# A decoder step on one core: cache keys of the decode part turned by VectorE in 32x32 blocks, scores in 32x32 tiles

## The chip, the core and the metric

The kernel runs on one of the eight cores of a Trainium2 chip. The metric is the time of one execution on the device in microseconds; before the change it is 4006.55 us, the median of three runs.

## What is computed

The reference is one inference step of a decoder layer for two inputs: a prompt of 2048 positions, and 8 sequences that decode 4 new positions each over a past of 8192. Both go through a projection, attention and an MLP; attention has two halves of four head pairs each. The decode part of attention, which the change touches, is cut here to its core:

```python
# dilated heads: keys at t, t-d, t-2d, ... of a window of the last 2048 positions
def dilated_branch_sample(q, k_all, v_all, window, dil):
    ...
    sc = jnp.einsum('nthe,ntjhe->nthj', q, kg).astype(jnp.float32) * (e ** -0.5)
    p, m, l = softmax_parts(sc, valid[None, :, None, :])
    o = jnp.einsum('nthj,ntjhe->nthe', p, vg.astype(jnp.float32)) / l
# differential heads: all keys of a paged cache, two maps per head
def diff_attention_core(q, k, v, valid, lam):
    sc = jnp.einsum('nqhce,nkhce->nhcqk', q, k).astype(jnp.float32) * (e ** -0.5)
    a = jax.nn.softmax(jnp.where(valid, sc, -jnp.inf), axis=-1)
    wts = a[:, :, 0] - lam * a[:, :, 1]
    return jnp.einsum('nhqk,nkhe->nqhe', wts, v.astype(jnp.float32))
```

A query row of decode is one of 4 positions, 4 head pairs and 2 heads or maps: 32 rows for each sequence and each half.

## The kernel before

The program has three stages one after the other: `project`, `attend` and `mlp`. All five engines are programmed by hand with semaphores; each carries out its own list in order.

`attend` does two things at once. The **prompt part** walks over units `u` (a tile of 128 queries; first 128 units of the dilated heads, then 64 of the differential heads) and their parts `j` of up to 512 keys. For each part TensorE makes scores (`scores`, L1000) for a unit that is two or three ahead, turns the probabilities of the present one (`turn_keys`, L1015) into one of the `turn` banks, and multiplies the copied ones with the values (`product`, L1050). VectorE adds the bias and takes the minimum (`biased`, L1394) and combines the two maps (`invert`, L1414), ScalarE does the exponentials (L1237) and copies turned tiles out of PSUM (`copies`, L1248; some of them fall to VectorE, `by_vector`).

The **decode part** walks over 8 sequences `n` and 9 chunks `c` of each: eight chunks of 8 pages of 128 cached positions for the differential heads, one chunk of eight 128-row groups of the window for the dilated ones; 72 chunks in all. For a chunk:
- SyncE loads the keys and GpSimd's queue the values in halves of 4 pages of 128 x 512 fp32 (rings `ck`, `cv` of three halves).
- TensorE turns the keys with 32 transposes of 128x128 (`turn_cache`, L1104), four to a bank; ScalarE (L1294) and VectorE (L1506) copy the banks in turn to `kT`.
- `cache_scores` (L1119) puts the scores into one bank: row 32 j + r is query row r against the keys of slot j (256 of the chunk's 1024 keys), summed over the four head pairs with queries that are zero outside their own head.
- VectorE takes the maximum of 256 columns (`maxima`, L1514, L1520, L1521), ScalarE the factor alpha for the old sum (L1303) and the exponentials (L1305).
- TensorE turns the 128x256 probabilities (`turn_prob`, L1130), ScalarE copies them (L1311), and `cache_values` (L1146) multiplies each slot with all 512 value columns; VectorE adds the result to `acc` (`add`, L1533).

Each query row so exists in four slots with its own maximum and sum. At the **edge** between two sequences (`edges`, seven steps) the four are brought to one maximum (L1156, L1160), their sums added (L1179), the finished sequence mixed (L1187), and the new positions' own keys scored (L1169) and their values taken (L1195, L1207).

The order between the two parts is fixed when the program is built. `pace` gives each prompt part a cost by its width and each decode step a cost from a table, and lays the decode steps between the parts so that both advance in proportion; every engine's list follows the same interleaving (`together`):

```python
turn, score, turn_p, value, edge = 0.46, 1.75, 0.3, 1.75, 1.0
chunk = [score, turn, turn, turn_p, turn, turn, value, turn, turn, turn, turn]
```

The turns of the next chunk's keys so stand between the steps of the present one.

Of the kernel before, what the change touches and what calls it, by code (L numbers as in the profile page):

```python
# [24 lines left out]
P = 128  # L25
# [404 lines left out]
SL = 4  # L430
# [4 lines left out]
def attend(nc, io, keep):  # L435
# [8 lines left out]
    TURNS, WB, OB, QB, KB, VB, CB = 3, 4, 2, 2, 6, 5, 5  # L444
    HK, HV = 3, 3
    H = CH // 2
    EV = NP * CH // 4
# [55 lines left out]
    def pace():  # L503
# [12 lines left out]
        turn, score, turn_p, value, edge = 0.46, 1.75, 0.3, 1.75, 1.0  # L516
        chunk = [score, turn, turn, turn_p, turn, turn, value, turn, turn, turn, turn]
        decode = [turn] * EV
        for n in range(ND + 1):
            decode += [edge] * 7 + (chunk * NC if n < ND else [])  # L520
# [21 lines left out]

    def chunk_after(n, c):
        return (n, c + 1) if c < NC - 1 else (n + 1, 0) if n < ND - 1 else None

    turn_keys_no, turn_inv_no, turn_coef_no, turn_cache_no, turn_prob_no, turn_new_no = {}, {}, {}, {}, {}, {}
# [9 lines left out]
    def by_vector(u, j, k):  # L556
        return not is_diff(u) and (k == 1 or (len(packs(u, j)) == 1 and u % 4 == 3))

    def count_prompt():
        for u in range(-AHEAD, NU):  # L560
            for j in steps(u):
# [3 lines left out]
                if u >= 0 and j < n_parts(u):  # L565
                    for k in range(len(packs(u, j))):
                        use(turn_keys_no, (u, j, k), 1 if by_vector(u, j, k) else 0)
                    if is_diff(u) and u % OT == OT - 1 and j == n_parts(u) - 1:
                        use(turn_inv_no, (u - DIFF0) // OT, 0)
                yield  # L570

    def count_decode():
        def turns(which, es):
            for e in es:
                if which is not None:
                    use(turn_cache_no, (*which, e), e % 2)
                yield
        yield from turns((0, 0), range(EV))
        for n in range(ND + 1):
            for edge in range(7):  # L580
                if edge == 4 and n < ND:
                    use(turn_new_no, n, 1)
                yield
            for c in range(NC if n < ND else 0):
                yield
                yield from turns(chunk_after(n, c), range(0, 2))
                use(turn_prob_no, (n, c), 0)
                yield
                yield from turns(chunk_after(n, c), range(2, 4))
                yield  # L590
                yield from turns(chunk_after(n, c), range(4, EV))
# [3 lines left out]
    with ExitStack() as ctx:  # L595
# [38 lines left out]
        kT = sb("c_kT", [P, NP, CH * P])  # L634
        q_rows = sb("c_q_rows", [P, 2, NP, SL * ROWS])
        v_new = sb("c_v_new", [TD, 2, GW])
        bias_new = sb("c_bias_new", [P, 2, TD])
        bias_win = sb("c_bias_win", [P, 2 * P])
        own_head = sb("c_own_head", [P, 2, GW])
        same_row = sb("c_same_row", [P, P])  # L640
        token = sb("c_token", [P, TD])
# [5 lines left out]
        s_win = sb("c_s_win", [P, 2 * P])  # L647
        m = sb("c_m", [P, 2, 2])
        chunk_max = sb("c_chunk_max", [P, 1])
        c_shift = sb("c_shift", [P, 2])  # L650
        shift_new = sb("c_shift_new", [P, 2])
        alpha = sb("c_alpha", [P, 2])
        l_new = sb("c_l_new", [P, 2])
        l_chunk = sb("c_l_chunk", [P, 2])
        l = sb("c_l", [P, 2])
        prob = [sb(f"c_prob{i}", [P, 2 * P]) for i in range(2)]
        pT = [sb(f"c_pT{i}", [P, 2 * P]) for i in range(2)]
        acc = sb("c_acc", [P, 2, GW])
        m_row = sb("c_m_row", [2, ROWS])
        m_rows = sb("c_m_rows", [2, SL, ROWS])  # L660
        below = sb("c_below", [P, 2])
        weight = sb("c_weight", [P, 2])
        lw = sb("c_lw", [P, 2])
        coef = sb("c_coef", [P, 2])
        comb = sb("c_comb", [P, 2, TD])
# [4 lines left out]
        cs_ps, co_ps = ps("c_s"), ps("c_o_ps")  # L670
        X_T = 2 * P
        X_M, X_L, X_O = X_T + P, X_T + P + 4, X_T + P + 8
# [29 lines left out]
        co_full, co_added, l_added = sem("c_o_full"), sem("c_o_added"), sem("c_l_added")  # L702
        new_scored, new_shifted, new_exped = sem("c_new_scored"), sem("c_new_shifted"), sem("c_new_exped")
# [1632 lines left out]
```

## Time and profile before

| | |
|---|---|
| three runs | 4004.82, 4006.55, 4008.26 us |
| profiled execution | 4008.4 us, span of its instructions 4006.8 us |
| TensorE (PE) busy | 3703.2 us, 92% |
| VectorE (DVE) busy | 2360.9 us, 59% |
| ScalarE (ACT) busy | 1570.7 us, 39% |
| mean granted TensorE clock | 0.957 |
| `attend` | about 741 to 2257 us |
| `mlp` | from 2257 us to the end |

PE's row counts matmuls, PEld the loading of their weights beside them. A group of instructions has a line, its tiles (written <- read), a count, its busy time and the idle time of the engine just ahead of it, with what ended that. The granted clock is a share of full speed.

### The profile page before, as it was taken

The page shows a single profiled execution, that of the slowest core. Times are in us where ns is not written, and L with a number is a line of the kernel's source. Part 1 is how long each engine was busy: PE and PEld are TensorE (multiplying, and loading weights), DVE is VectorE, ACT ScalarE, POOL GpSimd, SP SyncE. Part 2 cuts the span into 40 slices and gives each one's busy share as a digit, 9 for nine tenths or more (in the row PEclk, how much of TensorE's full clock was granted, in tenths as well). Part 3 has the DMA queues.
Part 4 walks back from the last instruction along what each step waited for, and adds up shares of the span by engine and source line. Part 5 has one row for each costly group of instructions (what it writes and reads, how often), then busy time and mean ns, then how long its engine had stood idle before and what let it go on. Part 6 is the DMA issues. An engine that isn't in the chain of part 4 may idle for free. (4 is left out here: it accounts for less than half of the span.)

```text
span 4006.8 us, 69226 instructions
## 1 busy us (share of the span) xinstructions
PE 3703.2 (92%) x24074; PEld 3143.2 (78%) x24074; DVE 2360.9 (59%) x5009; ACT 1570.7 (39%) x3039; POOL 356.3 (9%) x615
## 2 busy tenths in 40 slices
PE   7997799698989988989898699999999999999998
PEld 6885687466766666666666499999999999999998
DVE  4444343264555566666666566767767676676665
ACT  2222122253544443544444344444434434443433
POOL 0003000021212121222212000000000000000000
PEclk9998899698989998999989899999999999999999
DMA  5785763686868676867667344335434434433432
GB/s 176 250 280 176 262 220 109 189 277 205 281 199 285 210 267 205 277 198 281 213 224 240 112 150 134 115 114 155 119 93 150 136 104 139 146 114 110 140 113 70
DMA packets 529360, 725.20 MB, mean 181 GB/s; under 512 B 45688, under 2 KB 355192, under 8 KB 528025
## 3 DMA queue, kind: packets, MB, share of 16 engines
q1 hardware_dynamic: 480057, 502.32, 40.5%
q0 software_dynamic: 48128, 218.14, 15.9%
q8 instruction: 178, 2.92, 0.3%
q14 instruction: 133, 1.09, 0.1%
q10 hardware_dynamic: 864, 0.73, 0.1%
HBM read 653.30 MB, written 134.61 MB: 197 GB/s over the span
## 5 line engine op out<-in xcount | busy, mean ns | idle before, releaser
L2157 DVE TENSOR_TENSOR d_y<-d_y,d_dps 128x416 f32<-128x416 f32 x640 | 371.9, 586 | 246.5 <-PE d_dps L1822 246.5
L1820 PE MATMUL d_dps<-d_u_hi,d_down_hi 128*128 128x416 f32 x1280 | 459.1, 359 | 11.6 <-DVE d_y L2157 11.6
L1822 PE MATMUL d_dps<-d_u_hi,d_down_lo 128*128 128x416 f32 x1280 | 452.5, 353 | 0.0
L1822 PE MATMUL d_ups<-d_h_hi,d_up_lo 128*128 128x416 f32 x1280 | 451.0, 352 | 0.0
L1820 PE MATMUL d_ups<-d_h_hi,d_up_hi 128*128 128x416 f32 x1280 | 450.2, 352 | 0.0
L1821 PE MATMUL d_dps<-d_u_lo,d_down_hi 128*128 128x416 f32 x1280 | 448.8, 351 | 0.0
L1821 PE MATMUL d_ups<-d_h_lo,d_up_hi 128*128 128x416 f32 x1280 | 446.9, 349 | 0.0
L1104 PE MATMUL turn<-ident,c_k 128*128 128x128 f32 x2304 | 322.4, 281 | 42.5 <-DMA c_k<-in_k_cache 14.8
L761 POOL DMA_DIRECT2D c_v<-in_v_cache x512 | 276.8, 541 | 941.2 <-issue 941.2
L1104 PEld LDWEIGHTS turn<-ident,c_k 128*128 128x128 f32 x2304 | 256.4, 143 | 111.1 <-issue 51.4
L408 PE MATMUL a_zps<-a_w_hi,a_xT_hi 128*128 128x512 f32 (+1 forms) x816 | 330.3, 405 | 10.6 <-DVE a_w_lo L337 7.5
L410 PE MATMUL a_zps<-a_w_hi,a_xT_lo 128*128 128x512 f32 (+1 forms) x816 | 327.3, 401 | 0.0
L409 PE MATMUL a_zps<-a_w_lo,a_xT_hi 128*128 128x512 f32 (+1 forms) x816 | 324.9, 398 | 0.0
L1506 DVE COPY c_kT<-turn 128x512 f32<-128x512 f32 x288 | 197.7, 690 | 175.7 <-PE turn L1104 175.2
L2099 DVE TENSOR_TENSOR d_up_lo<-d_up_raw,d_up_hi 128x1024 fp32r<-128x1024 f32 x200 | 244.1, 1221 | 96.3 <-ACT d_up_hi L1943 96.1
L1248 ACT COPY b_wT<-turn 128x512 f32<-128x512 f32 (+2 forms) x264 | 138.7, 525 | 321.7 <-PE turn L1015 321.0
L1820 PEld LDWEIGHTS d_dps<-d_u_hi,d_down_hi 128*128 128x128 f32 x1280 | 241.6, 189 | 17.5 <-DVE d_y L2157 13.3
L1949 ACT CAST d_down_hi<-d_down_raw 128x2048 fp32r<-128x2048 f32 x80 | 152.7, 1908 | 253.9 <-PE d_dps L1822 253.6
L1943 ACT CAST d_up_hi<-d_up_raw 128x1024 fp32r<-128x1024 f32 x200 | 208.1, 1041 | 98.3 <-PE d_ups L1822 95.7
L1821 PEld LDWEIGHTS d_dps<-d_u_lo,d_down_hi 128*128 128x128 f32 x1280 | 241.8, 189 | 6.0 <-issue 2.6
L1821 PEld LDWEIGHTS d_ups<-d_h_lo,d_up_hi 128*128 128x128 f32 x1280 | 240.4, 188 | 4.4 <-issue 0.8
L1822 PEld LDWEIGHTS d_dps<-d_u_hi,d_down_lo 128*128 128x128 f32 x1280 | 241.3, 189 | 1.9
(215 smaller groups left out, 6759.2 us busy)
## 6 DMA issues: line engine op xcount, KB each, us to landing
c_v<-in_v_cache POOLq DMA_DIRECT2D x512, 256.0 KB, 5.2
c_k<-in_k_cache SPq DMA_DIRECT2D x512, 256.0 KB, 4.5
d_up_raw<-in_w_up SPq DMA_DIRECT2D x160, 512.0 KB, 4.3
d_down_raw<-in_w_down SPq DMA_DIRECT2D x80, 1024.0 KB, 5.5
out_ka_win<-in_ka_state POOLq DMA_DIRECT2D x8, 4064.0 KB, 15.5
out_va_win<-in_va_state POOLq DMA_DIRECT2D x8, 4064.0 KB, 27.1
d_up_raw<-in_w_out SPq DMA_DIRECT2D x40, 512.0 KB, 3.9
a_x<-in_x_prompt SPq DMA_DIRECT2D x32, 512.0 KB, 4.8
```

The lines of the kernel that those rows point to most:

```text
L408: nc.tensor.matmul(dst, x_hi, w_hi[i][:, c, :], start=(c == 0), stop=False)
L409: nc.tensor.matmul(dst, x_hi, w_lo[i][:, c, :], start=False, stop=False)
L410: m = nc.tensor.matmul(dst, x_lo, w_hi[i][:, c, :], start=False, stop=(c == KC - 1))
L761: eng.dma_start(dst[:, g, :], io[src[0]][bass.ds(page, 1)].rearrange("o p d -> (o p) d")).then_inc(landed, 16)
L1104: ins = nc.tensor.transpose(turn[n % TURNS][:, g * P:(g + 1) * P], ck[h % HK][:, g, p * P:(p + 1) * P], keep["ident"][:])
L1506: nc.vector.tensor_copy(kT[:, e % 4, e // 4 * 512:(e // 4 + 1) * 512], turn[n % TURNS][:]).then_inc(copied[1], 1)
L1820: nc.tensor.matmul(dst, w_hi, x_hi, start=first, stop=False)
L1821: nc.tensor.matmul(dst, w_hi, x_lo, start=False, stop=False)
L1822: return nc.tensor.matmul(dst, w_lo, x_hi, start=False, stop=last)
L1943: nc.scalar.copy(up_hi[n % UB][:], up_raw[n % 2][:]).then_inc(up_hi_ready, 1)
L2099: nc.vector.tensor_tensor(up_lo[n % UB][:], up_raw[n % 2][:], up_hi[n % UB][:].bitcast(F32), ALU.subtract).then_inc(up_lo_ready, 1)
L2157: nc.vector.tensor_tensor(part, part, d_ps[k % DB][:, 0:W], ALU.add).then_inc(d_used, 1)
```

## The change

Only the decode part of `attend` and its constants change.

- **Keys.** The 32 transposes and the 8 copies of a chunk go. VectorE turns the keys itself, from SBUF to SBUF, with four instructions of 128x1024 (`turn_cache`), each of which transposes all 32x32 blocks in place. Head dimension block x of a pair then lies on 32 partitions for each block k of 32 keys in a page.
- **Scores.** `cs_ps` has two banks. Each head pair has 32 rows of its own, of which 8 are used; each block k of 32 partitions holds a quarter of the keys. A score is summed over four 32x32 tiles x: 64 matmuls of 32 x 32 x 256 in place of 16 of 128 x 32 x 256. Blocks 0 and 2 come first, then, behind a wait of TensorE for its own half (`cs_half`), blocks 1 and 3.
- **Softmax.** A query row is one row, so slots have no longer to be joined. Maximum and exponentials run over 1024 columns instead of 256.
- **Values.** Eight transposes turn the 128x1024 probabilities; 32 matmuls of 128 x 32 x 128 take only the pair's own value columns; `acc` is 128x128 for each kind.
- **Edges** have four steps instead of seven; mixing takes two matmuls instead of eight.
- **Banks and order.** `TURNS` goes from 3 to 2, `by_vector` goes (ScalarE makes all copies of the prompt's turned tiles), and `pace` has a new table.

```diff
-    TURNS, WB, OB, QB, KB, VB, CB = 3, 4, 2, 2, 6, 5, 5
+    TURNS, WB, OB, QB, KB, VB, CB = 2, 4, 2, 2, 6, 5, 5
...
-        turn, score, turn_p, value, edge = 0.46, 1.75, 0.3, 1.75, 1.0
-        chunk = [score, turn, turn, turn_p, turn, turn, value, turn, turn, turn, turn]
+        edge = 1.5
+        chunk = [3.0, 1.5, 1.3, 1.0, 1.9, 0.5]
...
+    KEY_STEPS = (1, 2, 3, 5)
...
                 def cache_scores(n, c):
+                    i, kd = n * NC + c, kind(c)
+                    pe.wait_ge(keys_turned, EV * (i + 1))
+                    wait(pe, c_exped, i)
+                    for pair_of_blocks in ((0, 2), (1, 3)):
+                        for x in range(4):
+                            for k in pair_of_blocks:
+                                rows = slice(k * BLK, (k + 1) * BLK)
+                                for p in range(NP):
+                                    at = (p * 4 + x) * BLK
+                                    ins = nc.tensor.matmul(
+                                        cs_ps[ROWS * p:ROWS * (p + 1), k * 2 * P:(k + 1) * 2 * P],
+                                        q_rows[rows, kd, p, x, :], kT[rows, :, at:at + BLK],
+                                        start=(x == 0), stop=(x == 3))
+                        if pair_of_blocks == (0, 2):
+                            ins.then_inc(cs_half, 1)
+                            pe.wait_ge(cs_half, i + 1)
+                    ins.then_inc(cs_full, 1)
...
-                    for p in range(NP):
-                        for j in range(SL):
-                            ins = nc.tensor.matmul(
-                                cs_ps[ROWS * j:ROWS * (j + 1), 0:2 * P],
-                                q_rows[:, kind(c), p, ROWS * j:ROWS * (j + 1)],
-                                kT[:, p, j * 2 * P:(j + 1) * 2 * P], start=(p == 0), stop=(p == NP - 1))
...
-                    for a in range(2):
-                        for j in range(SL):
-                            g = 2 * j + a
+                    for g in range(CH):
+                        for p in range(NP):
                             ins = nc.tensor.matmul(
-                                co_ps[ROWS * j:ROWS * (j + 1), :], pT[i % 2][:, a * P + ROWS * j:a * P + ROWS * (j + 1)],
-                                cv[(2 * i + g // H) % HV][:, g % H, :], start=(a == 0), stop=(a == 1))
+                                co_ps[ROWS * p:ROWS * (p + 1), 0:P], pT[:, g * P + ROWS * p:g * P + ROWS * (p + 1)],
+                                cv[(2 * i + g // H) % HV][:, g % H, p * P:(p + 1) * P], start=(g == 0), stop=(g == CH - 1))
...
+                def turn_cache(which, e):
...
+                    i = which[0] * NC + which[1]
+                    h = i * 2 + e // 2
+                    if e % 2 == 0:
+                        dve.wait_ge(ck_in[h % HK], half_landed(h, HK))
+                    wait(dve, cs_full, i)
+                    pages = slice(e % 2 * 2, e % 2 * 2 + 2)
+                    nc.vector.transpose(kT[:, e * 2:e * 2 + 2, :].rearrange("p g d -> p (g d)"),
+                                        ck[h % HK][:, pages, :].rearrange("p g d -> p (g d)")).then_inc(keys_turned, 1)
...
                     if kd:
-                        link(nc.vector.tensor_reduce(chunk_max[:], cs_ps[:, 0:2 * P], AX.X, ALU.max))
+                        link(nc.vector.tensor_reduce(chunk_max[:], cs_ps[:], AX.X, ALU.max))
```

How this moves TensorE's list shows chunk 60, in the differential half: from its scores (`c_s`) to its turned probabilities. `b_` names are the prompt part. Before:

```order
L1119 MATMUL c_s<-c_kT,c_q_rows 32x256 x16
L1000 MATMUL b_s<-b_k_hi,b_q_hi 128x384 x2
L1000 MATMUL b_s<-b_k_lo,b_q_hi 128x384 x2
L1000 MATMUL b_s<-b_k_hi,b_q_lo 128x384 x2
L1015 MATMUL turn<-ident,b_w 128x128
L1050 MATMUL b_ops<-b_wT,b_v 128x128 x4
L1104 MATMUL turn<-ident,c_k 128x128 x8
L1000 MATMUL b_s<-b_k_hi,b_q_hi 128x512 x2
...
L1015 MATMUL turn<-ident,b_w 128x128 x4
L1050 MATMUL b_ops<-b_wT,b_v 128x128
L1130 MATMUL turn<-ident,c_prob 128x128 x2
```

and after:

```order
L1089 MATMUL c_s<-c_kT,c_q_rows 32x256 x64
L984 MATMUL b_s<-b_k_hi,b_q_hi 128x512 x2
L984 MATMUL b_s<-b_k_lo,b_q_hi 128x512 x2
L984 MATMUL b_s<-b_k_hi,b_q_lo 128x512 x2
L999 MATMUL turn<-ident,b_w 128x128 x4
L1034 MATMUL b_ops<-b_wT,b_v 128x128
L1106 MATMUL turn<-ident,c_prob 128x128 x8
```

Eight key transposes and one of the two prompt parts no longer stand between the two. The second place is VectorE's list at the end of the same chunk, up to the maximum of the next one. Before:

```order
L1533 SCALAR_TENSOR_TENSOR c_acc<-c_acc,c_alpha,c_o_ps 128x512 [waits c_o_full]
L1394 ISA b_w,b_part<-b_s,b_bias_causal 128x512 [waits b_s_full]
L1394 ISA b_part 128x1
...
L1506 COPY c_kT<-turn 128x512 [waits c_s_full,turned] x2
L1394 ISA b_w,b_part<-b_s,b_bias_causal 128x512 [waits b_s_full]
...
L1514 TENSOR_REDUCE c_chunk_max<-c_s 128x1 [waits c_s_full]
```

and after:

```order
L1489 SCALAR_TENSOR_TENSOR c_acc<-c_acc,c_alpha,c_o_ps 128x128 [waits c_o_full]
L1350 ISA b_w,b_part<-b_s,b_bias_causal 128x512 [waits b_s_full]
L1350 ISA b_part 128x1
...
L1454 STREAM_TRANSPOSE c_kT<-c_k 128x1024 [waits c_s_full]
L1462 TENSOR_REDUCE c_chunk_max<-c_s 128x1 [waits c_s_full]
```

The last key transpose now stands directly ahead of the maximum, behind the prompt part's tiles; TensorE's scores of the next chunk wait for it.

## Rows read from the trace of the kernel before

**Rows 1.** Busy time by stretch: us, each engine busy (x instructions), granted clock, DMA share, GB/s.
```profile
741.00:1395.00 654.00, 597.92 (x5563) 422.01 (x5563) 354.04 (x1115) 297.78 (x900) 124.32 (x229) 0.91 0.74 236
1395.00:2257.00 862.00, 766.67 (x6503) 547.19 (x6503) 535.36 (x1548) 386.55 (x796) 181.26 (x333) 0.94 0.69 231
741.00:2257.00 1516.00, 1364.59 (x12066) 969.20 (x12066) 889.40 (x2662) 684.33 (x1696) 305.58 (x562) 0.93 0.71 233
2257.00:4007.00 1750.00, 1694.67 (x9010) 1660.80 (x9010) 1171.24 (x1569) 726.38 (x1061) 0.00 (x0) 0.98 0.41 124
```

**Rows 2.** Groups by line, PE, 741 to 2257 us: busy us, mean ns, idle before, releasers.
```profile
L1104 PE MATMUL turn<-ident,c_k 128*128 128x128 f32 x2304 | 322.4, 281 | 42.5 <-DMA c_k<-in_k_cache 14.8 <-DVE c_kT L1506 8.4 <-ACT c_kT L1294 8.3
...
L1119 PE MATMUL c_s<-c_kT,c_q_rows 128*32 128x256 f32 x2304 | 144.7, 393 | 37.7 <-issue 29.4 <-ACT c_kT L1294 8.3
L1146 PE MATMUL c_o_ps<-c_v,c_pT 128*32 128x512 f32 x1152 | 138.5, 598 | 0.4 <-ACT c_pT L1311 0.4
...
L1130 PE MATMUL turn<-ident,c_prob 128*128 128x128 f32 x144 | 29.2, 284 | 16.6 <-ACT c_prob L1305 9.1 <-ACT b_wT L1248 6.2 <-ACT c_kT L1294 0.9
L1207 PE MATMUL c_o_ps<-c_v_new,c_pT_new 4*128 4x512 f32 x32 | 28.8, 994 | 14.9 <-DVE c_acc L1623 12.1 <-DVE c_pT_new L1617 2.8
L1187 PE MATMUL c_s<-c_comb,c_acc 128*128 128x4 f32 x128 | 23.2, 313 | 2.1 <-DVE c_comb L1602 2.1
...
L1169 PE MATMUL c_s<-ksT,c_q_rows 128*128 128x4 f32 x128 | 21.8, 302 | 6.0 <-DVE c_below L1576 6.0
```

**Rows 3.** Timeline of PE from 2230 us: start us, us, engine, line, tiles, xcount.
```profile
2230.46 1.93 PE L1119 MATMUL c_s<-c_kT,c_q_rows 128*32 128x256 f32 x32 [0.83 <-ACT c_kT L1294]
2232.32 0.50 PE L1000 MATMUL b_s<-b_k_hi,b_q_hi 64*128 64x512 f32 x2
...
2233.22 0.44 PE L1015 MATMUL turn<-ident,b_w 128*128 128x128 f32 x2
2233.49 1.06 PE L1050 MATMUL b_ops<-b_wT,b_v 128*128 128x128 f32 x8
...
2238.64 1.92 PE L1146 MATMUL c_o_ps<-c_v,c_pT 128*32 128x512 f32 x16
```

**Rows 4.** Timeline of PE from 747 us, eight transposes of keys at full clock.
```profile
747.61 1.04 PE L1104 MATMUL turn<-ident,c_k 128*128 128x128 f32 x8
```

**Rows 5.** Groups by line, DVE, 741 to 2257 us.
```profile
L1506 DVE COPY c_kT<-turn 128x512 f32<-128x512 f32 x288 | 197.7, 690 | 175.7 <-PE turn L1104 175.2
L1394 DVE CUSTOM_DVE_ANT_0 b_w<-b_s,b_bias_causal 128x512 f32<-128x512 f32 x224 | 145.7, 688 | 37.1 <-PE b_s L1000 33.0 <-issue 0.5
...
L1533 DVE SCALAR_TENSOR_TENSOR c_acc<-c_acc,c_alpha,c_o_ps 128x512 f32<-128x512 f32 x72 | 53.7, 746 | 77.7 <-PE c_o_ps L1146 77.5
...
L1514 DVE TENSOR_REDUCE c_chunk_max<-c_s 128x1 f32<-128x256 f32 x64 | 27.2, 424 | 108.1 <-PE c_s L1119 108.1
...
L1520 DVE TENSOR_TENSOR c_m<-c_m,c_chunk_max 128x1 f32<-128x1 f32 x72 | 11.5, 160 | 2.5
...
L1581 DVE TENSOR_TENSOR c_acc<-c_acc,c_own_head 128x1024 f32<-128x1024 f32 x8 | 9.7, 1218 | 0.0
```

**Rows 6.** Groups by line, ACT, 741 to 2257 us.
```profile
L1294 ACT COPY c_kT<-turn 128x512 f32<-128x512 f32 x288 | 167.5, 584 | 163.5 <-PE turn L1104 161.3
L1248 ACT COPY b_wT<-turn 128x512 f32<-128x512 f32 x184 | 107.4, 583 | 230.9 <-PE turn L1015 230.4
...
L1305 ACT ACTIVATE c_prob<-c_s,c_shift 128x256 f32<-128x256 f32 x64 | 29.2, 456 | 0.0
...
L1303 ACT ACTIVATE c_alpha<-c_m,c_shift 128x1 f32<-128x1 f32 x72 | 21.2, 295 | 241.3 <-DVE c_shift L1521 241.3
...
L1237 ACT ACTIVATE b_w<-b_w,b_shift 128x1024 f32<-128x1024 f32 x8 | 9.2, 1153 | 0.0
```

**Rows 7.** Timeline of 0.12 us at the start of the same score group.
```profile
2230.43 0.19 PEld L1119 LDWEIGHTS c_s<-c_kT,c_q_rows 128*32 128x32 f32 x8 [1.04 <-ACT c_kT L1294]
2230.46 0.42 PE L1119 MATMUL c_s<-c_kT,c_q_rows 128*32 128x256 f32 x4 [0.83 <-ACT c_kT L1294]
```

More of the change, by code:

```diff
@@ L429 @@
 CH = 8
-SL = 4
 ROWS = 32
@@ L572, in count_decode @@
     def count_decode():
[L573 to L578, printed above, removed]
+        for e in range(EV):
+            yield
         for n in range(ND + 1):
-            for edge in range(7):
-                if edge == 4 and n < ND:
+            for edge in range(EDGES):
+                if edge == 2 and n < ND:
                     use(turn_new_no, n, 1)
@@ L584, in count_decode @@
             for c in range(NC if n < ND else 0):
[L585 to L591, printed above, removed]
+                for step in range(6):
+                    if step == 2:
+                        for a in range(2):
+                            use(turn_prob_no, (n, c, a), 0)
+                    yield
     together(count_prompt(), count_decode())
@@ L652, in attend @@
         alpha = sb("c_alpha", [P, 2])
-        l_new = sb("c_l_new", [P, 2])
         l_chunk = sb("c_l_chunk", [P, 2])
         l = sb("c_l", [P, 2])
[L656 to L663, printed above, removed]
+        prob = sb("c_prob", [P, CH * P])
+        pT = sb("c_pT", [P, CH * P])
+        acc = sb("c_acc", [P, 2, P])
         coef = sb("c_coef", [P, 2])
-        comb = sb("c_comb", [P, 2, TD])
+        comb = sb("c_comb", [P, 2, NP * TD])
         s_ps = [ps(f"b_s{i}") for i in range(2)]
@@ L1132, in turn_prob @@
-                    ins.then_inc(turned, 1)
+                        t = turn_prob_no[n, c, a]
+                        after_copy(pe, t - TURNS)
+                        for g in range(H):
+                            at = (a * H + g) * P
+                            ins = nc.tensor.transpose(turn[t % TURNS][:, g * P:(g + 1) * P], prob[:, at:at + P],
+                                                      keep["ident"][:])
+                        ins.then_inc(turned, 1)
                 def cache_values(n, c):
@@ L1286, in prompt @@
                             yield
-                def copy_keys(which, es):
-                    for e in es:
-                        if which is not None and e % 2 == 0:
-                            i, n = which[0] * NC + which[1], turn_cache_no[(*which, e)]
-                            act.wait_ge(turned, n + 1)
-                            wait(act, cs_full, i)
-                            nc.scalar.copy(kT[:, e % 4, e // 4 * 512:(e // 4 + 1) * 512], turn[n % TURNS][:]).then_inc(copied[0], 1)
-                        yield
                 def cache_exps(n, c):
```

370 lines of the change are left out of this document (155 added, 215 removed).

## Prediction

> **What bounds the kernel now.** I read the stretches first [rows 1]. The attention stage, from 741 to 2257 us, is the only one that the change touches: 1516 us, TensorE (PE) busy for 1365 of them, VectorE (DVE) 889, ScalarE (ACT) 684, DMA at 0.71. In its first 654 us the dilated heads of the prompt run beside 30 of the 72 chunks of cache, in the other 862 us the differential heads beside 42 chunks. The stage after it, 1750 us, stays as it is. So PE's time in the stage is what has to be summed, with a check whether DVE, which takes work over, becomes the one waited for. The groups of PE's lines say what the decode part costs there [rows 2]; the timeline says how long one such piece lasts at full clock [rows 3, 4]; DVE's and ACT's groups price their pieces [rows 5, 6].
>
> **PE, what goes.** Busy time and the idle time ahead of it count together [rows 2]. The 2304 transposes of cache keys (L1104): 322.4 + 42.5 = 365 us. The scores (L1119): 144.7 + 37.7 = 182. The values (L1146): 139. The transposes of probabilities (L1130): 29.2 + 16.6 = 46. The edges between sequences, their three large groups (L1207, L1187, L1169): 43.7 + 25.3 + 27.8 = 97; the small ones are left out on both sides. Together 829 us.
>
> **PE, what comes.** An fp32 matmul is two passes in the trace (1152 score matmuls in the program, 2304 records). Today 32 passes of 256 columns, on four column groups at a time, take 1.93 us [rows 3], and one pass takes 393 ns [rows 2]: eight waves, so a wave costs (1.93 - 0.39) / 7 = 0.22 us. The changed scores are 64 matmuls of 32x32, 128 passes. They are written so that row groups 0 and 2, then 1 and 3, work beside each other on four column groups: eight tiles at a time, 16 waves. The wait on c_s_half in the middle cuts them into two blocks of eight waves, each as long as today's block: 3.86 us. With the entry of 37.7 / 72 = 0.52 us that is 4.38 us a chunk, 315 us. If the row groups don't overlap it is 32 waves (a rival below). The values stay four tiles wide, 64 passes of 128 columns instead of 16 of 512; the columns streamed are the same, so I take the same 139 us. Probabilities: eight transposes instead of two, 1.04 us [rows 4], 75 us. Edges: two mixing matmuls for eight (a quarter of 25.3 us), half of the 28 us of the new scores, and about half of the 44 us of the new values, since two round trips to DVE become one: 6 + 14 + 24 = 44 us. Together 573 us. Without new waits PE gains 829 - 573 = **256 us**.
>
> **What the waits take back.** The cache transposes were also filler: PE did them while DVE and ACT worked on the scores. The order of chunk 60 shows it: between its scores and its turned probabilities stand now two prompt parts and eight key transposes, afterwards one part with a single product. Take T as the end of the scores.
> - DVE's maximum over 1024 columns instead of 256: copies and products of 512 and 1024 columns differ by (1218 - 690) / 512 = 1.03 ns a column [rows 5], so 424 + 768 x 1.03 = 1.22 us, then two small operations of 0.16 us (L1520 and one like it). ACT then needs 0.30 us for alpha and about 1.15 us for 1024 exponentials, as its 1024-column row [rows 6]. The probabilities are there at T + 3.1 us, against 0.42 + 0.32 + 0.30 + 0.46 = T + 1.5 now.
> - PE's one part is 0.90 us of scores, four transposes of 0.11 (eight take 1.04) and two passes of 0.11 of product [rows 3, 4]: T + 1.6. It waits 1.5 us.
> - DVE goes on: two biased tiles of 0.69 us with their read-outs (1.5), two key transposes, one more part, a third transpose, the sum. The 128x1024 transpose of 32x32 blocks is in no row. The nearest is L1581, a 128x1024 operation from SBUF to SBUF at 1218 ns; the bounds are 0.69 us (the 512-column copy) and 2.44 us (two passes over the data). I take 1.22. That brings DVE to T + 9, the next part's tiles to T + 10.7, the fourth transpose to T + 11.9. PE, which has done turned probabilities, part, values and part, stands at T + 10.4 and waits 1.5 us for c_keys_turned. What is queued behind that wait on PE is the whole prompt.
>
> So a tight chunk of three parts pays 3.0 us. A chunk has 4.4 parts on average (315 parts, 72 chunks), and where a second part stands in the gap the wait goes. I take 2.0 us a chunk, 144 us; bounds 0.5 (36 us, hardly more than the 16.6 us that L1130 waits now) and 3.5 us (252 us).
>
> **DVE and the rest.** DVE loses the key copies (288 x 0.69 = 198 us) and gains 288 x 1.22 = 351, loses 0.4 and gains 1.22 us a chunk on the maximum, and its sum shrinks from 0.75 to about 0.3 us a chunk. With some of the prompt's copies going to ACT (each 0.58 us there, [rows 6]) it ends near 1000 of some 1400 us. It also idles while PE does scores, today 108 us [rows 5], then some 3.7 us a chunk, 270 us: nearly full in the second half, which is why I don't take the low bound of the waits. ACT loses 168 us of key copies [rows 6] and gains less than that: no cost; it only adds to waits where a long prompt exponential stands ahead. Two transpose buffers instead of three cost nothing, because the third held key tiles; were that cover missing, a part would pay a copy of 0.58 us. The key loads (SP) now wait for DVE's transposes, the value loads (POOL) for the same values as before; nothing else stands behind them, and DMA goes from 0.71 to 0.76 of its time.
>
> **Sum.** The profiled execution took 4008.4 us for a span of 4006.8, 1.9 us above the median of the three runs. 4008.4 - 256 + 144 = **3896 us**. Its own range, from the bounds of the waits: 3788 to 4004.
>
> **Rivals.**
> - **Row groups don't overlap.** Each half of the scores then has 16 waves: 2 x (15 x 0.22 + 0.39) = 7.4 us, 3.5 more a chunk, +253: **4149 us**, slower. For it: no row shows two 32-row tiles at work. Against it: today's prompt scores use two 64-row groups, and two matmuls of 512 columns are done within 0.50 us there [rows 3], where a single wave of 512 columns in fp32 takes 0.44. It decides as soon as a block of 32 matmuls lasts over 2.9 us. The Trainium skill (TensorEngine Tiling (Array Packing), Gotcha 1: PSUM Pressure) says that different row tiles cannot use one PSUM bank at once. By it nothing is lost here, since blocks 0 and 2 write to different halves of a two-bank tile; no run so far shows it. Chance 0.10.
> - **PE's issue binds.** If 1.93 / 32 = 60 ns a pass is the rate at which instructions come, and not that of the array, the scores take 128 x 0.06 = 7.7 us and the values 3.8: +276 and +138 us, **4310 us**. Against it: eight weight loads and four matmuls start within 0.12 us [rows 7]. The Trainium skill (TensorE: Matmul & The Clock Gate, Part 2) gives about 62 ns of sequencer time per matmul with hardware decode off; by that rule the scores would need 7.9 us. Row and rule differ, and I follow the row. Chance 0.03.
> - **The DVE transpose costs two passes, 2.44 us.** In the tight chunk the fourth transpose ends 4.6 us later and PE waits for it; over a mean chunk I take 3 us, +216: **4112 us**, slower. It decides from about 1.9 us for one transpose. The Trainium skill (Vector Engine (DVE) Microarchitecture Reference, 3.8) says that the transpose sustains one element per cycle and lane, which is on the side of my 1.22 us; no row shows it. Chance 0.12.
> - **Every chunk is tight**, with an exponential of the prompt in front as well: 3.5 us a chunk, **4004 us**, no change. Chance 0.06.
>
> **How the numbers follow.** The forecast has 0.69. A measurement of this kernel can tell about 0.2% (8 us) from no change. Faster: 0.69. Within 0.2%: 0.05 of the last rival. Slower: 0.10 + 0.03 + 0.12 + 0.01 = 0.26. The range runs from the forecast's low end, 3785, to just over the third rival, 4120; it leaves out the first two rivals and a little below, under 0.2.
>
> **What would show it.** Right: the 128-pass score group at some 3.9 us, blocks of eight matmul starts together; the DVE transpose near 1.2 us; PE idle ahead of c_prob and of c_s, waiting for c_prob (ACT) and c_kT (DVE), 2 us a chunk together; a stage of about 1404 us. Wrong: a score group over 6 us, a transpose over 1.9 us, waits beyond 3.5 us a chunk, or a granted clock below the present 0.93 in the stage. The stage of 1750 us should not move.

## The result and the profile after

| | before | changed |
|---|---|---|
| median | 4005.7 us (4 runs) | 4098.7 us (4 runs) |
| span of the profiled execution | 4006.8 us | 4101.7 us |
| attention stage | 1516 us | 1613 us |
| TensorE busy, idle in it | 1365, 151 us | 1353, 260 us |
| granted clock in it | 0.93 | 0.84 |

The changed kernel is slower: ratio 1.0235, interval 1.0214 to 1.0257. Here and below a ratio is that of medians, against the kernel before as measured beside the run, with its 95% interval; those medians of the kernel before lie between 4005.2 and 4007.9 us. The forecast was 3896 us. The profiled execution took 4103.3 us; 207 us are missing.

The stretches after, with the columns of [rows 1]:

```profile
741.00:1395.00 654.00, 566.62 (x8566) 401.49 (x8566) 367.36 (x1037) 275.01 (x816) 117.90 (x218) 0.82 0.71 227
1395.00:2354.00 959.00, 786.53 (x11950) 581.09 (x11946) 640.63 (x1598) 367.49 (x706) 186.38 (x344) 0.86 0.64 215
741.00:2354.00 1613.00, 1353.15 (x20510) 982.59 (x20510) 1007.99 (x2635) 642.51 (x1520) 304.29 (x562) 0.84 0.67 220
2354.00:4102.00 1748.00, 1694.71 (x9010) 1660.80 (x9010) 1170.85 (x1566) 726.03 (x1061) 0.00 (x0) 0.98 0.41 123
```

The last stage did not move. In the attention stage TensorE is busy for 12 us less, where the sum had 173 less, and the granted clock is 0.84 instead of 0.93. PE's groups after, 741 to 2354 us (to compare with [rows 2]):

```profile
L1089 PE MATMUL c_s<-c_kT,c_q_rows 32*32 32x256 f32 x9216 | 348.0, 441 | 55.3 <-DVE c_kT L1454 41.5 <-issue 4.8 <-PE c_s L1089 0.3
L999 PE MATMUL turn<-ident,b_w 128*128 128x128 f32 x1112 | 214.7, 322 | 29.7 <-DVE b_w L1370 16.0 <-DVE b_o_near L1401 8.6 <-ACT c_pT L1268 2.8
L1034 PE MATMUL b_ops<-b_wT,b_v 128*128 128x128 f32 x1088 | 174.4, 308 | 7.4 <-ACT b_wT L1208 7.2
L1122 PE MATMUL c_o_ps<-c_v,c_pT 128*32 128x128 f32 x4608 | 145.6, 280 | 10.0 <-ACT c_pT L1268 8.7 <-issue 1.3
L1106 PE MATMUL turn<-ident,c_prob 128*128 128x128 f32 x576 | 95.3, 313 | 25.6 <-ACT c_prob L1260 14.0 <-ACT b_wT L1208 11.4
L984 PE MATMUL b_s<-b_k_hi,b_q_hi 64*128 64x512 f32 x248 | 72.2, 574 | 51.1 <-DVE b_part L1350 42.4 <-DVE b_shift L1350 7.7 <-DVE b_both L1350 0.9
...
L1166 PE MATMUL c_o_ps<-c_v_new,c_pT_new 4*32 4x128 f32 x128 | 7.1, 352 | 4.3 <-DVE c_pT_new L1555 4.3
L1146 PE MATMUL c_o_ps<-c_comb,c_acc 128*128 128x16 f32 x32 | 6.9, 334 | 12.8 <-DVE c_comb L1543 12.8
...
L1135 PE MATMUL c_o_ps<-ksT,c_q_new 128*32 128x4 f32 x128 | 3.0, 194 | 39.1 <-DVE c_q_rows L1514 39.1
```

The reader is to see three things. The prompt's own groups, which the change did not touch, take longer: turning the prompt's probabilities (L999, before L1015) 214.7 us for 195.9, the products 174.4 for 155.3. TensorE now waits for DVE in many places: for keys (41.5), for bias tiles (b_part, 42.4 for 11.3 before), and for c_q_rows, the copies of the queries at the edges (39.1). The kernel before makes such copies too, 16 a sequence, but there they keep DVE busy for half as long, and TensorE never waits for them:

```profile
L1558 DVE COPY c_q_rows<-qsT 64x16 f32<-64x16 f32 x128 | 11.5, 174 | 0.3
```

And the scores are 348 us where the sum had 278 without their entry.

The timeline of PE after, two chunks:

```profile
2220.07 6.57 PE L1089 MATMUL c_s<-c_kT,c_q_rows 32*32 32x256 f32 x128 [2.00 <-DVE c_kT L1454]
2241.92 4.04 PE L1089 MATMUL c_s<-c_kT,c_q_rows 32*32 32x256 f32 x128
```

and the first 0.13 us of the second group:

```profile
2241.92 0.44 PE L1089 MATMUL c_s<-c_kT,c_q_rows 32*32 32x256 f32 x8
```

Eight tiles start together, so row groups do overlap. At full clock a group takes 4.04 us, near the 3.86 of the sum; the other one took 6.57 us, because the clock fell while it ran: TensorE is busy from 2220.07 us on, with a granted clock of 0.66 up to 2223.00 and of 0.50, the low level (1.2 GHz), from there to 2226.60. DVE's groups after, 741 to 2354 us, the counterparts of [rows 5], and ACT's exponential of [rows 6]:

```profile
L1454 DVE STREAM_TRANSPOSE c_kT<-c_k 128x1024 f32<-128x1024 f32 x286 | 346.6, 1231 | 7.8 <-DMA c_k<-in_k_cache 7.5 <-issue 0.3
...
L1462 DVE TENSOR_REDUCE c_chunk_max<-c_s 128x1 f32<-128x1024 f32 x64 | 78.4, 1225 | 288.8 <-PE c_s L1089 288.8
L1489 DVE SCALAR_TENSOR_TENSOR c_acc<-c_acc,c_alpha,c_o_ps 128x128 f32<-128x128 f32 x72 | 25.0, 347 | 81.4 <-PE c_o_ps L1122 81.3
...
L1514 DVE COPY c_q_rows<-qsT 32x32 f32<-32x32 f32 x128 | 22.6, 177 | 1.6
```

```profile
L1260 ACT ACTIVATE c_prob<-c_s,c_shift 128x1024 f32<-128x1024 f32 x64 | 70.1, 1095 | 0.0
```

The block transpose takes 1.23 us and the maximum 1.23 us, as priced; DVE idles 289 us in front of the maximum, as priced (270).

**Where the 207 us are**, by groups (busy; idle ahead), the profile after against the sum. In the rows on waits c_s and c_prob stand for the groups of the scores and of the turned probabilities:

| term | sum | measured | difference |
|---|---|---|---|
| scores, busy | 278 | 348 | +70 |
| prompt's 18 groups, busy | 875, as before | 943 | +68 |
| turned probabilities and values | 75 + 139 | 95 + 156 | +37 |
| edges | 44 | 73 | +29 |
| waits: c_s, c_prob, and what the prompt's groups wait more than their 28 us before | 38 + 144 | 55 + 26 + 78 | -23 |
| overlap: the groups' busy times add up to more than PE's | 0 | 232 before, 200 after | +32 |
| small groups of the edges, left out on both sides | 0 | 26 before, 5 after | -21 |
| a wait for the first keys, ahead of 741 us | -13 | 0 | +13 |

The overlap is an error of method. Each matmul group starts before the one ahead has drained, so the groups of before sum to 1597 us where PE was busy for 1365; a part of what I took away group by group was never there to gain. The last row is a misreading: of the 42.5 us of idle time taken away with L1104, 12.9 lie before the stage begins, and the changed kernel waits there for something else.

```profile
740.92 1.11 PE L1104 MATMUL turn<-ident,c_k 128*128 128x128 f32 x4 [12.93 <-DMA c_k<-in_k_cache]
```

The eight rows make 205 us; the rest is rounding and some 1 us of the last stage.

### The profile page after: what moved, and what is told of

Read it like the earlier page. It is cut to its first block and busy times, and to the rows that moved or that the text cites. A ratio compares the mean times of both kernels' runs of the same rounds, so it can differ in the third digit from the quotient of the medians.

```text
span 4101.7 us, 85450 instructions
## 1 busy us (share of the span) xinstructions
PE 3694.1 (90%) x32530; PEld 3158.1 (77%) x32530; DVE 2482.6 (61%) x4986; ACT 1530.5 (37%) x2871; POOL 354.9 (9%) x615
## 5 line engine op out<-in xcount | busy, mean ns | idle before, releaser
L1759 PE MATMUL d_dps<-d_u_hi,d_down_hi 128*128 128x416 f32 x1280 | 458.8, 358 | 11.3 <-DVE d_y L2096 11.3
L1089 PE MATMUL c_s<-c_kT,c_q_rows 32*32 32x256 f32 x9216 | 348.0, 441 | 55.3 <-DVE c_kT L1454 41.5
L1454 DVE STREAM_TRANSPOSE c_kT<-c_k 128x1024 f32<-128x1024 f32 x288 | 349.1, 1231 | 15.6 <-DMA c_k<-in_k_cache 15.3
L1089 PEld LDWEIGHTS c_s<-c_kT,c_q_rows 32*32 32x32 f32 x9216 | 181.9, 118 | 190.5 <-issue 53.0
L1208 ACT COPY b_wT<-turn 128x512 f32<-128x512 f32 (+3 forms) x320 | 164.8, 526 | 320.7 <-PE turn L999 320.1
L1462 DVE TENSOR_REDUCE c_chunk_max<-c_s 128x1 f32<-128x1024 f32 x64 | 78.4, 1225 | 288.8 <-PE c_s L1089 288.8
```

Of the source, the lines that this page charges most:

```text
L1089: ins = nc.tensor.matmul(cs_ps[ROWS * p:ROWS * (p + 1), k * 2 * P:(k + 1) * 2 * P], q_rows[rows, kd, p, x, :], kT[rows, :, at:at + BLK], s ...
L1454: nc.vector.transpose(kT[:, e * 2:e * 2 + 2, :].rearrange("p g d -> p (g d)"), ck[h % HK][:, pages, :].rearrange("p g d -> p (g d)")).then ...
L1759: nc.tensor.matmul(dst, w_hi, x_hi, start=first, stop=False)
```

## The experiments

Theories first. **A**: the granted clock fell because the 32-row score tiles hold half of the array while they run. **B**: it fell because TensorE now stands in waits that the key transposes used to fill. What TensorE waits for is a question apart.

**pad64.** 64-row tiles; the half of the weights that belongs to the other block is zero.

```diff
-rows = slice(k * BLK, (k + 1) * BLK)
+rows = slice(k // 2 * HD, (k // 2 + 1) * HD)
-q_rows[rows, kd, p, x, :], kT[rows, :, at:at + BLK]
+q_rows[rows, k % 2, kd, p, x, :], kT[rows, :, at:at + BLK]
```

> The changed kernel with its scores in tiles of 64 rows instead of 32: the weights of the other block's 32 rows are zero, the same 64 matmuls, the same eight tiles at a time, the same waits, the same scores; only the rows of the array that a tile takes are doubled (all 16 of its 32x32 parts instead of 8). Theory A (the granted clock of the attention stage fell from 0.93 to 0.84 because the score tiles hold only half of the array for 3.9 us a chunk): clock of the stage back to 0.91 to 0.94, TensorE's busy time in it down by 90 to 130 us, time about 3990 (3970 to 4010). Theory B (it fell because TensorE now stands in waits of 110 us more, which the key transposes used to fill): clock stays at 0.84, time 4090 to 4105. Score group 3.9 us in both.

Measured: 4055.6 us, ratio 1.0115 (1.0098 to 1.0132). Its stage, and the groups of PE in it, 741 to 2306 us:

```profile
741.00:2306.00 1565.00, 1262.71 (x20510) 939.24 (x20510) 1007.54 (x2635) 641.03 (x1520) 304.29 (x562) 0.91 0.69 227
```

```profile
L1089 PE MATMUL c_s<-c_kT,c_q_rows 64*32 64x256 f32 x9216 | 305.3, 400 | 55.2 <-DVE c_kT L1454 41.5 <-issue 4.6 <-PE c_s L1089 0.5
L999 PE MATMUL turn<-ident,b_w 128*128 128x128 f32 x1112 | 199.9, 305 | 37.0 <-DVE b_w L1370 19.8 <-DVE b_o_near L1401 9.2 <-ACT c_pT L1268 4.8
...
L1106 PE MATMUL turn<-ident,c_prob 128*128 128x128 f32 x576 | 92.4, 305 | 41.2 <-ACT c_prob L1260 23.4 <-ACT b_wT L1208 17.6
```

The clock went from 0.84 to 0.91 and busy time fell by 90 us, as theory A had it, with the very same waits in the program. The first score group of the stage shows it by itself. In the changed kernel TensorE is busy in it from 766.2 to 773.7 us, and the granted clock is 0.50 throughout; in pad64 it is 0.53 for the group's first 3.55 us and 1.00 for its last 1.96. B is out as the cause of this fall: TensorE is idle for 302 us here, more than the 260 of the changed kernel, and has the higher clock. But the time fell by 43 us only, outside A's range: 42 of the 90 us came back as idle time, because a faster TensorE reaches DVE's and ACT's results sooner (c_prob 14.0 to 23.4 us). The Trainium skill (TensorE: Matmul & The Clock Gate, What's actually happening) says that the gate follows how busy the engine has recently been. In the trace's sense of busy this pair goes the other way: 0.84 of the stage busy at clock 0.84, 0.81 busy at 0.91.

**full_rows.** The scores as 32 matmuls of 128 rows, four at a time.

```diff
-for k in pair_of_blocks:
+k = pair_of_blocks[x // 2]
...
-q_rows[rows, kd, p, x, :], kT[rows, :, at:at + BLK],
-start=(x == 0), stop=(x == 3))
+q_rows[:, kd, p, x, :], kT[:, :, at:at + BLK],
+start=(x % 2 == 0), stop=(x % 2 == 1))
```

> The changed kernel with its scores as 32 matmuls of all 128 rows and 32 columns, four at a time, two blocks of eight waves as now. What they compute is not the scores of the kernel; probabilities and values go on from them. Theory A: as pad64, clock 0.91 to 0.94 and time 3970 to 4010. Theory B: 4090 to 4105. If pad64 does not raise the clock and this does, it is rows with data that count, not rows that a tile takes (theory C).

Measured: 4045.3 us (1.0094, 1.0077 to 1.0111), clock 0.91 in the stage. The time is above A's range again. Rows filled with data do no more for the clock than pad64's rows of zeros, so theory C is out.

**before_32_rows.** The reverse, on the kernel before.

```diff
-q_rows[:, kind(c), p, ROWS * j:ROWS * (j + 1)],
-kT[:, p, j * 2 * P:(j + 1) * 2 * P], start=(p == 0), stop=(p == NP - 1))
+q_rows[0:ROWS, kind(c), p, ROWS * j:ROWS * (j + 1)],
+kT[0:ROWS, p, j * 2 * P:(j + 1) * 2 * P], start=(p == 0), stop=(p == NP - 1))
```

> The kernel before with its 16 score matmuls a chunk over the first 32 rows of queries and keys instead of all 128: the same number of matmuls, columns, waits and key transposes, so the same 1.93 us a chunk, with a quarter of the array. The scores lack three quarters of their sum. Theory A: the clock of the stage falls, from 0.93 to 0.89 to 0.91 (half as long as the change's scores, a quarter of the array), time 4030 to 4075. Theory B: nothing moves, clock 0.93, 3995 to 4012.

Measured: 4035.9 us (1.0077, 1.0058 to 1.0096). Its stage:

```profile
741.00:2281.00 1540.00, 1404.09 (x12062) 998.35 (x12060) 889.79 (x2665) 687.32 (x1696) 304.52 (x562) 0.90 0.71 230
```

With all key transposes and waits of the kernel before in place, 32-row tiles alone lower the clock from 0.93 to 0.90 and cost 29 us. That is A's direction and size.

**prob_turned_twice.**

```diff
-for g in range(H):
+for g in (*range(H), *range(H)):
```

> The changed kernel with its eight transposes of probabilities done twice, 1.04 us of full-array work more on TensorE in each of 72 chunks, 75 us in all (the same outputs). Theory A: the clock rises a little, to 0.85 to 0.87, which gives back 20 to 40 us; time 4110 to 4160. Theory B (filler is what is missing): the clock rises to 0.88 or more, and the time stays at 4080 to 4110 in spite of 75 us more work.

Measured: 4123.1 us (1.0290, 1.0273 to 1.0307), clock 0.87. 75 us of full-array work cost 24 us: busy time rose by 24 only, since the rest ran faster. A's numbers; the filler as such is not what is missing.

**pad64_no_wait.**

```diff
-if pair_of_blocks == (0, 2):
-    ins.then_inc(cs_half, 1)
-    pe.wait_ge(cs_half, i + 1)
```

> pad64 without the wait on c_s_half between the two blocks of scores, which 64-row tiles do not need (blocks 0 and 1 lie on the same rows). Theory D (each of the two blocks pays its pipeline once, 0.39 us a chunk): scores 3.5 to 3.6 us instead of 3.9 to 4.2, time 20 to 30 us under pad64, 4025 to 4035. Rival: DVE is as late as before, so what the scores save comes back as a longer wait for keys or for bias tiles: within 8 us of pad64, 4048 to 4064.

Measured: 4033.4 us (1.0069, 1.0053 to 1.0084), 22 us under pad64. Its timeline has the group at full clock as

```profile
2219.03 3.69 PE L1089 MATMUL c_s<-c_kT,c_q_rows 64*32 64x256 f32 x128
```

against 4.05 in pad64: 0.36 us x 72 = 26 us. Theory D holds in the time and at full clock, though 3.69 is a little more than the 3.5 to 3.6 expected; over all 72 groups the scores' busy time fell by 13 us only, from 305.3 to 292.4.

**pad64_queries_early.**

```diff
+if c == NC - 1 and n < ND - 1 and 1 <= step <= 4:
+    queries(n + 1, (step - 1,))
```

> pad64 with the 20 copies of a sequence's queries taken out of the edge, five in each of steps 1 to 4 of the last chunk of the sequence before it. Theory E (the prediction priced the edges' round trip but not these copies: 40 us of TensorE's idle time stand ahead of the new scores): that wait falls from 40 to under 15 us, time 25 to 35 us under pad64, 4020 to 4031. Rival: the copies now delay DVE's key transposes and the wait shows up at c_kT instead: within 8 us of pad64.

Measured: 4045.9 us (1.0103, 1.0088 to 1.0119), 10 us under pad64. The wait itself went as expected, from 40.3 to 11.7 us, but most of it was paid elsewhere (c_comb 12.8 to 21.7 us, and bias tiles). That lies between the two forecasts. Half right: the copies were an uncosted wait, but worth 10 us by the medians, not 30 (the profiled execution alone, with a span of 4029.6 us, was 24 under pad64's).

**pad64_keys_ahead** and **split_only.** The first splits the scores by pages and puts a key transpose between; the second splits the matmuls only.

```diff
+for half in range(2):
...
+at, to = (p * 4 + x) * BLK, k * 2 * P + half * P
-cs_ps[ROWS * p:ROWS * (p + 1), k * 2 * P:(k + 1) * 2 * P],
+cs_ps[ROWS * p:ROWS * (p + 1), to:to + P],
-q_rows[rows, k % 2, kd, p, x, :], kT[rows, :, at:at + BLK],
+q_rows[rows, k % 2, kd, p, x, :], kT[rows, half * H:(half + 1) * H, at:at + BLK],
```

In pad64_keys_ahead alone, TensorE waits for each half of the keys by itself, and of DVE's steps (the one of step 0 stands ahead of the maximum):

```diff
-wait(dve, cs_full, i)
+wait(dve, cs_full if e // 2 else cs_half, i)
-KEY_STEPS = (1, 2, 3, 5)
+KEY_STEPS = (0, 1, 2, 3)
```

> pad64 with the scores split by pages: first the 128 columns of the first four pages for all four blocks, then the other four, no wait between; DVE turns the first two pages of the next chunk's keys in between, ahead of the maximum instead of behind it, and the others one step earlier. Theory F (what costs the waits is the lock step: DVE stands idle for 3.9 us of scores in every chunk, 250 us, and its 349 us of key transposes are packed into the rest): DVE's idle time ahead of the maximum falls by 80 us or more, TensorE's idle time in the stage from 298 to 220 or less, time 3965 to 4005. Rival G (DVE is in time, and the waits are the chain scores, maximum, exponential, turned probabilities alone): only the saved c_s_half wait counts, 4025 to 4050.

> pad64_no_wait with each score matmul of 256 columns as two of 128 (128 matmuls a chunk instead of 64), all keys waited for ahead of them, DVE's order untouched. Theory I (the hole in pad64_keys_ahead is TensorE's instructions not arriving fast enough, since a group now has 512 of them; the idle time is put down to issue and to no wait): the same hole of 2.9 us, idle time ahead of the scores 180 to 200 us, time 4200 to 4250. Theory J (it came from the key transposes being ahead, by a wait on them): no hole, 4030 to 4060.

Measured: pad64_keys_ahead 4238.4 us (1.0579, 1.0563 to 1.0595), far on the wrong side of both theories. split_only 4324.6 us in a single run, so with no interval. PE's timeline in split_only:

```profile
2006.99 2.82 PE L1090 MATMUL c_s<-c_kT,c_q_rows 64*32 64x128 f32 x183 [0.23 <-DVE c_kT L1452]
...
2014.30 2.36 PE L1090 MATMUL c_s<-c_kT,c_q_rows 64*32 64x128 f32 x73 [4.49 <-issue]
...
2029.66 2.64 PE L1090 MATMUL c_s<-c_kT,c_q_rows 64*32 64x128 f32 x172 [1.70 <-DVE c_kT L1452]
2037.36 2.77 PE L1090 MATMUL c_s<-c_kT,c_q_rows 64*32 64x128 f32 x84 [5.06 <-issue]
```

Here are the same columns as in pad64, in twice the instructions, and a hole of 4 to 5 us after some 160 to 220 of 256 matmul records, in which no wait ends. Such holes are in most groups of both kernels: 79 in split_only, of 0.3 to 5.5 us and 227 us together, and 86 with 220 us in pad64_keys_ahead. So they are there with the key transposes ahead or not: J is out, and of I stands that the number of matmuls brings them, at a larger price than I gave it (4200 to 4250). The queues of DMA in the hole, 2009.8 to 2014.3 us, show one packet of instructions (the queue's 236 packets in this stage move 3.87 MB, 16 KB each):

```profile
q8 instruction: 1, 0.02, 1.3%
```

That instructions arrive too late is the reading that fits; it was not shown by itself, and the packet is weak evidence, as one comes every 8 us on average. The Trainium skill (Runtime: NRT & Kernel Launch, Instruction fetch mechanics) says that an engine fetches its program in blocks of 16 KiB and that this is mostly hidden; here, if the reading is right, it is not. The lock-step theory F could not be judged by the pair alone. Its sign did not come: DVE's idle time ahead of the maximum fell from 250.9 us in pad64 to 230.9 in pad64_keys_ahead, not by 80, and 161 us of new idle time stand ahead of the key transposes; but the holes lengthen both. Still, with the same matmuls, the kernel with the earlier key transposes was 86 us faster, by the one run of split_only.

**all_three.** pad64_keys_ahead with early queries.

> The three together: 64-row tiles, pages in halves with a key transpose ahead of the maximum, queries early. If theories A, D, E and F hold and add up: 3930 to 3975, faster than the kernel before. If F is wrong: 4000 to 4020.

Measured: 4222.2 us (1.0540, 1.0514 to 1.0567), 16 us under pad64_keys_ahead. It holds the same hole and settles nothing more.

**short_key_turns.**

```diff
-pages = slice(e % 2 * 2, e % 2 * 2 + 2)
+pages = slice(e % 2 * 2, e % 2 * 2 + (1 if i else 2))
```

> pad64_no_wait with each of DVE's key transposes over one page of two from the second chunk on: 284 operations of 512 columns instead of 1024, some 0.62 us less each, 175 us less DVE work; half of kT keeps the first chunk's keys, so scores, probabilities and values are not the kernel's. Theory F' (most of TensorE's 288 us of idle time in the stage is DVE being late, because its key transposes stand ahead of bias tiles and of the next scores): idle time falls by 90 us or more, time 3930 to 3960. Rival G (the idle time is the latency of the chain scores, maximum, exponential, turned probabilities): it falls by under 40 us, time 3995 to 4025.

Measured: 3987.7 us (0.9955, 0.9939 to 0.9971), 46 us under pad64_no_wait. Between the profiled executions, 51 us apart, TensorE's idle time falls by 30 us and its busy time by 19. Half-wide transposes took 697 ns, so DVE lost some 150 us of work. Idle time in G's range, time between the two: taking half of the transposes' work from DVE removes 30 of TensorE's 288 us of idle time. F' is out as the main cause; latency and order are left.

**no_wait_and_queries, more_in_the_gap, fourth_turn_sooner.** The first has the edits of pad64_no_wait and pad64_queries_early together; more_in_the_gap adds the first of these lines to it, fourth_turn_sooner the second.

```diff
-chunk = [3.0, 1.5, 1.3, 1.0, 1.9, 0.5]
+chunk = [3.0, 3.0, 1.3, 1.0, 1.9, 0.5]
...
-KEY_STEPS = (1, 2, 3, 5)
+KEY_STEPS = (1, 2, 3, 4)
```

> The two parts that helped, together: 64-row tiles without the wait between the blocks of scores, and queries copied early. If they add up: 4033 less 10 to 25, so 4008 to 4023, no faster than the kernel before.

> no_wait_and_queries with step 1 of a chunk (between scores and turned probabilities) counted as 3.0 instead of 1.5 in the table that lays prompt parts among the steps: more prompt work between scores and turned probabilities, less elsewhere. If the chain scores, maximum, exponential is what TensorE waits for, the wait at c_prob falls from 23 to under 10 us and the time by 10 to 30 us. If DVE is late for everything (F'), the wait only changes its place: within 8 us of no_wait_and_queries.

> no_wait_and_queries with the fourth key transpose in step 4 instead of step 5, before the last parts of the chunk and with the sum. If the fourth transpose is what the scores wait for (my tight chunk in the prediction): the wait at c_kT falls from 39 to under 20 us and the time by 10 to 20 us. If it is then paid at bias tiles (F'): within 8 us.

Measured: 4022.6 us (1.0043, 1.0031 to 1.0055); 4009.9 us (1.0011, 1.0002 to 1.0020); 4002.8 us (0.9995, 0.9984 to 1.0005). PE's groups of scores and turned probabilities, 741 to 2275 us, first in no_wait_and_queries:

```profile
L1089 PE MATMUL c_s<-c_kT,c_q_rows 64*32 64x256 f32 x9216 | 287.0, 397 | 47.9 <-DVE c_kT L1451 41.5 <-issue 5.9
...
L1103 PE MATMUL turn<-ident,c_prob 128*128 128x128 f32 x576 | 92.9, 306 | 40.8 <-ACT c_prob L1257 22.0 <-ACT b_wT L1205 18.2
```

in more_in_the_gap:

```profile
L1103 PE MATMUL turn<-ident,c_prob 128*128 128x128 f32 x576 | 91.7, 303 | 22.0 <-ACT c_prob L1257 12.4 <-ACT b_wT L1205 9.1
```

and in fourth_turn_sooner:

```profile
L1089 PE MATMUL c_s<-c_kT,c_q_rows 64*32 64x256 f32 x9216 | 278.9, 388 | 15.9 <-DVE c_kT L1451 11.1 <-issue 4.4
```

Both waits shrink where their cause was taken away (22.0 to 12.4, which is short of the "under 10" expected, and 41.5 to 11.1), and the time falls by 13 and 20 us. With the fourth transpose sooner this is idle time: TensorE's falls by 18 us in the stage, its busy time by 2. So that one is a wait of order, a key transpose that starts too late, which the prediction named. The other gain has a second source. In more_in_the_gap the wait for keys grows,

```profile
L1089 PE MATMUL c_s<-c_kT,c_q_rows 64*32 64x256 f32 x9216 | 282.6, 392 | 51.0 <-DVE c_kT L1451 47.0 <-issue 3.7
```

and idle time in all falls by 5 us only; busy time falls by 15, as the stage's granted clock goes from 0.91 to 0.93. The profiled execution was the fastest of its ten, so a part of this may be that execution's own. Why the clock moves with the order wasn't tested.

**both_orders, both_orders_wider, order_with_32_rows.** Both lines at once; the same with a wider table; and both lines with early queries on the changed kernel's 32-row tiles. The table of the second:

```diff
-chunk = [3.0, 3.0, 1.3, 1.0, 1.9, 0.5]
+chunk = [3.0, 3.0, 1.3, 1.0, 2.5, 1.5]
```

> no_wait_and_queries with both changes of order: more prompt work in the gap, and the fourth key transpose in step 4. If their gains (13 and 20 us) add: 3985 to 3995, faster than the kernel before by some 0.4%. If the wait only moves on once one of them is in: 4000 to 4006.

> both_orders with steps 4 and 5 counted as 2.5 and 1.5 instead of 1.9 and 0.5, so that more prompt work stands between the values and the next scores as well, and less beside the scores and the middle steps. If it is room before the next scores that DVE lacks: 5 to 15 us under both_orders. If the table is near its best: within 8 us, or slower.

> The changed kernel (32-row tiles, the wait between the blocks of scores) with queries early and both changes of order. If order and clock are separate costs: the order gives about as much as with 64-row tiles (10 + 33 us), 4050 to 4070, and the clock of the stage stays at 0.84 to 0.86. If at the low clock DVE has time enough and order matters less: 4070 to 4090.

Measured: 3992.9 us (0.9967, 0.9954 to 0.9980); 3991.0 us (0.9959, 0.9944 to 0.9975); 4051.1 us (1.0111, 1.0093 to 1.0129). The stages of both_orders and of order_with_32_rows:

```profile
741.00:2239.00 1498.00, 1230.83 (x20516) 944.81 (x20514) 1006.91 (x2636) 640.56 (x1524) 304.30 (x562) 0.93 0.72 237
```

```profile
741.00:2298.00 1557.00, 1309.88 (x20513) 966.17 (x20510) 1007.14 (x2636) 642.42 (x1522) 304.66 (x562) 0.88 0.69 228
```

The gains of the two orders add up (30 us of 33), about half of it in idle time and half in busy time (18 and 16 us of the stage against no_wait_and_queries), and the table is near its best. With 32-row tiles the order gives about as much (48 us with the queries), while clock and busy time stay behind: 58 us lie between the two, 22 of them the wait between the blocks. The clock did rise there, to 0.88, above the 0.86 that I allowed: order and clock are not separate costs. both_orders computes what the changed kernel computes and is 0.3% faster than the kernel before.

## Why the prediction was wrong

- **The step that failed: the granted clock, taken as it was.** The sum priced every group by durations at today's clock and had no term for the clock itself; it stood only among what would prove it wrong. pad64 puts its price at 90 us of busy time, 43 us of time with the waits as they were. It is the largest single cause found. It isn't the whole: pad64 still is 1.15% slower than the kernel before, and its stage is some 158 us over the sum's. By the rows of the table these are 38 of overlap, 34 of probabilities and values, 30 of edges, 27 of scores, 20 of waits, 17 of the prompt's groups and 13 of the first keys' wait, less the 21 of small groups. So the sum would have missed the sign with the clock in it. Scores in tiles of a quarter of the rows were costed by their length alone, 3.86 us; at full clock they took 4.04, and 4.83 on average (348 / 72).
- **Edges.** Priced by TensorE's groups [rows 2], 44 us; 73 measured, 39 of them behind the 20 small copies of queries a sequence on DVE (16 x 8 = 128 of them c_q_rows, 177 ns each), which the sum did not list. Such copies were there before, with no wait of TensorE behind them; what is new is their price, 28 us of DVE with the copies to c_q_new for 11.5, and that TensorE's next step waits for them. Worth 10 us when taken away.
- **Taking away by groups.** Group times overlap: 32 us of the difference could not be gained, nor could the 13 us of the wait ahead of the stage; the small groups of the edges, left out, give 21 back. One must take the difference of PE's busy time, not add groups.
- **Values and probabilities.** 37 us over: 10 are a new wait for the copy of c_pT. Low clock is little of the rest, since pad64, at 0.91, still has 92.4 us of turned probabilities and 146.8 of values. The sum took the full-clock 1.04 us for every group of eight transposes, where the mean of before was 1.12 (322.4 / 288). What remains isn't explained.
- **Waits.** 144 us were taken; with the scores' entry that makes 182 against 159 measured in the changed kernel and 202 in pad64. Right in size, and the two named waits are there: 41.5 us for c_kT, 25.6 ahead of the turned probabilities, each under the 1.5 us a chunk of the tight case. Half of the measured sum lies elsewhere, most of it ahead of the prompt's own scores, which wait for DVE's bias tiles. More of it was a matter of order than I saw: two numbers in the program give back 30 us, a part of them by the clock.
- **DVE.** Transpose 1.23 us for 1.22, maximum 1.23 for 1.22, busy 1008 for about 1000, idle ahead of the maximum 289 for 270. All right.
- **Rivals.** Row groups overlap; the issue of instructions does not bind at 64 matmuls a group. The DVE transpose is not two passes. "Every chunk is tight" is out too: with the scores' entry it needs 252 + 38 us of waits, and 159 were measured. None of the four contained the clock, so the range held the result, 4099, by the luck of another rival's 4112.

Still open: why the stage's clock also rises with the order of the work, from 0.84 to 0.88 with 32-row tiles. And what share of the 86 us between split_only and pad64_keys_ahead is the lock step of DVE and TensorE. A second buffer for the turned keys would tell; it wasn't tried. That the hole in split_only is a late block of instructions is argued, not shown.

## What to carry to other kernels

Before a full-array matmul is replaced by small tiles, put a term for the granted clock into the sum, over all that runs in that stage; if the tiles leave rows unused, zero-padded weights on taller tiles cost no time of their own and got 43 us back here. Work that is taken off the engine that bounds was also cover for the chains beside it: move the parts that lie in the gaps along with it, and take differences of the engine's busy time, not of its groups. And cost the small copies of a moved step on the engine that issues them.

## What the runs showed of the hardware

- Eight 32x32 or 64x32 tiles work at once into two PSUM banks: at full clock 16 waves of 256 columns take 4.04 us with a wait in the middle, and in 64x32 tiles 3.69 without it.
- The granted clock of the stage went with the rows that the score tiles take: 0.84 with 32 rows, 0.91 with 64 and with 128; on the kernel before 0.93 with 128 and 0.90 with 32. Rows with zero weights count like others. The order of the work moved it too, less: 0.84 to 0.88 with 32 rows, with early queries and both changes of order, and 0.91 to 0.93 with 64 in both_orders.
- A DVE transpose of 32x32 blocks, 128x1024 in fp32, takes 1231 ns, and 697 ns for 512 columns: about 1.04 ns a column, like a copy.
- 256 matmul records with their weight loads in one group, 128 columns each, ran into 79 holes of 0.3 to 5.5 us put down to issue, 227 us in 72 groups (split_only); groups of 128 records of 256 columns had 5 us of it in all (pad64).
